# A decoder layer's projections: the products with the weights' high part first, those with the low part last

## The reference

```python
xn = rms_norm(x, attn_norm_w)
q, k, v, qi, ki, wi, cx, cb, cc, ga, gc = split(xn @ w_in)
q, k = rope(rms_norm(q)), rope(rms_norm(k)); qi, ki = rope(qi), rope(ki)
attn = attend(q, k, v, qi, wi, ki)        # keys picked by top-256 of the indexer's scores
conv_out = cb * causal_dwconv([conv_prev, cc * cx], conv_w)
mixed = sigmoid(ga) * (attn @ w_o_attn) + sigmoid(gc) * (conv_out @ w_o_conv)
h = x + mixed @ w_merge
g, val = split(rms_norm(h) @ w_up)
y = h + (silu(causal_dwconv(g) + b) * val) @ w_down
```

## Time and profile before

| | us |
|---|---|
| time, median of 3 runs | 1758.48 |
| lowest and highest run | 1755.22, 1758.77 |
| the profiled execution's own time | 1760.87 |
| its span, first to last instruction | 1759.0 |
| PE busy in the span | 1685.2 |
| DVE busy | 1240.5 |
| ACT busy | 695.2 |
| POOL busy | 879.6 |

### The profile page before, as it was taken

One profiled execution on the slowest core, in us unless ns is written; L12 is line 12 of the kernel. 1 busy time (PEld: TensorE's weight loads), 2 busy tenths in 40 slices (PEclk: granted clock), 3 DMA queues, 4 the chain that ended last, 5 costly groups with the idle time before them and its releaser, 6 DMA issues.

```text
span 1759.0 us, 31969 instructions
## 1 busy us (share of the span) xinstructions
PE 1685.2 (96%) x11519; PEld 1620.4 (92%) x11519; DVE 1240.5 (71%) x1957; ACT 695.2 (40%) x1054; POOL 879.6 (50%) x466
## 2 busy tenths in 40 slices
PE   7999999999999889999799998899999999999999
PEld 5858999999999778898799998899999999999999
DVE  5569999999899655556543378677777776655555
ACT  4755552232111377777212334344444444311110
POOL 2504762455786556755221224666666666633331
PEclk9999999999999889899999999999999999999999
DMA  5221112111776242222333312212222122622222
GB/s 196 83 71 37 36 48 87 60 54 56 267 238 210 67 142 76 85 74 91 114 133 133 142 64 84 73 72 95 72 72 84 72 82 87 240 96 96 96 77 96
DMA packets 66978, 178.32 MB, mean 101 GB/s; under 512 B 15386, under 2 KB 15514, under 8 KB 66762
## 3 DMA queue, kind: packets, MB, share of 16 engines
q1 hardware_dynamic: 56786, 140.91, 24.1%
q10 hardware_dynamic: 9392, 32.10, 4.8%
q0 software_dynamic: 720, 4.29, 0.6%
HBM read 141.79 MB, written 35.58 MB: 101 GB/s over the span
## 4 chain that ended last, share of the span: by engine, by line
PE 75%; DVE 11%; ACT 3%; issue 3%; POOL 3%; SPq 3%; DMA 2%; DVEq 0%; ACTq 0%; POOLq 0%
PE PS L1075 16%; PE PS L663 15%; PE PS L1139 11%; PE PX L1075 6%; PE PS L998 5%; PE PS L1043 5%; PE PX L1139 4%; PE PS L951 3%; DVE S L2108 2%; DVE M L2106 2%; PE PS L921 2%; PE PX L934 2%; DVE LD L2088 2%; PE PS L979 2%; PE PS L766 1%
## 5 line engine op out<-in xcount | busy, mean ns | idle before, releaser
L663 PE MATMUL PS<-XH,WHI 128*128 128x346 f32 (+1 forms) x984 | 321.4, 327 | 6.2 <-POOL WLO L1741 4.9
L663 PE MATMUL PS<-XL,WHI 128*128 128x346 f32 (+1 forms) x984 | 318.1, 323 | 0.0
L663 PE MATMUL PS<-XH,WLO 128*128 128x346 f32 (+1 forms) x984 | 317.5, 323 | 0.0
L1741 POOL TENSOR_TENSOR WLO<-WRAW,WHI 128x1024 fp32r<-128x1024 f32 x58 | 143.7, 2478 | 296.7 <-ACT WHI L1167 296.6
L2108 DVE MATCH_REPLACE8 S<-M,S 128x1024 f32<-128x1024 f32 (+3 forms) x224 | 206.0, 926 | 0.0
L663 PEld LDWEIGHTS PS<-XH,WHI 128*128 128x128 f32 x984 | 186.6, 190 | 16.1 <-issue 9.3
L2106 DVE MAX8 M<-S 128x8 f32<-128x1024 f32 (+3 forms) x224 | 200.7, 931 | 0.4
L663 PEld LDWEIGHTS PS<-XH,WLO 128*128 128x128 f32 x984 | 186.6, 190 | 0.0
L663 PEld LDWEIGHTS PS<-XL,WHI 128*128 128x128 f32 x984 | 186.6, 190 | 0.0
L2382 DVE TENSOR_TENSOR HY<-HY,PS 128x344 f32<-128x344 f32 x198 | 100.9, 513 | 79.2 <-PE PS L1139 79.2
L1139 PE MATMUL PS<-FH,DLO 128*128 128x344 f32 x396 | 126.7, 320 | 0.0
(11 more groups left out here) (369 smaller groups left out, 4821.0 us busy)
## 6 DMA issues: line engine op xcount, KB each, us to landing
WRAW<-wtiles SPq DMA_DIRECT2D x49, 512.0 KB, 3.6
KR<-cache_k SPq DMA_DIRECT2D x64, 256.0 KB, 3.0
RING<-cache_v SPq DMA_DIRECT2D x64, 256.0 KB, 2.9
ffn_act<-TG ACTq DMA_DIRECT2D x22, 516.0 KB, 2.7
FRAW<-ffn_act SPq DMA_DIRECT2D x11, 1032.0 KB, 6.9
RAWG<-wtiles SPq DMA_DIRECT2D x22, 512.0 KB, 3.6
RAWV<-wtiles SPq DMA_DIRECT2D x22, 512.0 KB, 4.4
DRAW<-wdown SPq DMA_DIRECT2D x11, 1024.0 KB, 4.9
```

The lines of the kernel that those rows point to most:

```text
L663: last = nc.tensor.matmul(PS[b][:, c, 0:n], w[b][:, kk, :], x[:, kk, t0 + c * n:t0 + (c + 1) * n], start=(kk == 0 and p == 0), stop=(kk == ...
L1741: nc.gpsimd.tensor_tensor(WLO[b][:, :, :], WRAW[b][:, :, :], WHI[b][:, :, :].bitcast(F32), ALU.subtract).then_inc(w_lo[b], 1)
```

## The change

`proj` waits for the high part of its weights (`w_hi`) where it waited for the low part. It runs the 16 products with the high part for each of the three chunks, 48 in all, then waits for `w_lo`, and then runs the 24 products with the low part, again chunk by chunk. `mid` and `mid1` are still called behind the first and the second chunk of the first loop, so they stand behind 16 and 32 matmuls where they stood behind 24 and 48. Number and shapes of the matmuls are as before.

```diff
-                pe.wait_ge(w_lo[b], k + 1)
+                pe.wait_ge(w_hi[b], k + 1)
                 if not (isinstance(k, int) and k == 0):
                     pe.wait_ge(ps_free[b], k)
                 if extra:
                     extra()
                 for c in range(NCH):
                     for kk in range(kn):
-                        for p, (w, x) in enumerate(((WHI, xh), (WHI, xl), (WLO, xh))):
-                            last = nc.tensor.matmul(PS[b][:, c, 0:n], w[b][:, kk, :], x[:, kk, t0 + c * n:t0 + (c + 1) * n],
-                                                    start=(kk == 0 and p == 0), stop=(kk == kn - 1 and p == 2))
+                        for p, x in enumerate((xh, xl)):
+                            nc.tensor.matmul(PS[b][:, c, 0:n], WHI[b][:, kk, :], x[:, kk, t0 + c * n:t0 + (c + 1) * n],
+                                             start=(kk == 0 and p == 0), stop=False, skip_group_check=True)
                     if c == 0 and mid:
                         mid()
                     if c == 1 and mid1:
                         mid1()
+                pe.wait_ge(w_lo[b], k + 1)
+                for c in range(NCH):
+                    for kk in range(kn):
+                        last = nc.tensor.matmul(PS[b][:, c, 0:n], WLO[b][:, kk, :], xh[:, kk, t0 + c * n:t0 + (c + 1) * n],
+                                                start=False, stop=(kk == kn - 1), skip_group_check=True)
                 last.then_inc(mm[b], 1)
```

## The result

The changed kernel takes 1761.24 us (median of 17 runs: 16 from 1757.68 to 1767.29 us, and a disturbed one of 5312.67 us, which the comparison leaves out); the kernel before, run beside it, 1756.65 us (17 runs, 1752.5 to 1758.89). The ratio is 1.0024 [1.0016, 1.0033]: slower by 0.24%, some 4.2 us. Forecast were 1759.6 us and +1.1 us. The time lies in the range and the sign is right, but the loss is three to four times the forecast, and just beyond the 0.2% within which the forecast called it no change (its likeliest outcome, 0.71). That the time is only 1.6 us from the forecast one is in part luck: before's median is 1756.65 us over 17 runs, 1.83 us under the 1758.48 from which the forecast counted.

A forecast was written before the change was run, and what follows sets the result against it. PE was taken to set the pace until the convolution's results are written, DVE's searches later, to 596 us. -3.33 + 0.3 + 2.56 + 1.55 = +1.1 us on the median 1758.48 gave 1759.6 us, range 1756.0 to 1763.0.

The forecast's parts named there:

- Part one: PE's wait at 142.28 us: 1.87 us goes by the moved `weigh_past`, 1.46 by the slow clock behind it; 3.33 gained.
- Part two: The eight `head_sums` move up 8 matmuls and may wait for ACT's squares; 0.3 us lost.
- The early gain: PE's time saved before 437 us brings key pages and DVE forward; 3.0 us, DVE's result at 595.5 instead of 598.5.
- slower rival: The gain before the first key pages never reaches DVE, which ends at 598.5 as before; 1762.6 us, chance 0.16.
- Part four: Behind DVE's last result: 40 matmuls instead of 24 follow `decode_logits`, 2.56 us, and an earlier slow clock, 1.55; 4.1 lost.
- Part three: Removing the low-part waits at 459.31 and 576.08 us is worth nothing: PE only waits longer for DVE, 8.7 us.
- Faster: Rival: all four low-part waits (4.93 us) and two slow stretches come off in full; 7.9 us, 1750.6, chance 0.09.
- Nothing happens: Rival: the low part is almost always there first, gain and loss each under a microsecond; 1758.5 us, chance 0.09.

The follow-up runs named there:

- e4: The changed kernel (new order, moved guests), but with the low part waited for ahead of the whole projection; ratio 1.0000 against the kernel before.
- e7: The kernel before, with the new order only in the one projection that holds `weigh_past`; ratio 0.9987 against the kernel before.
- e1: The kernel before, with the new order only in the last projection; ratio 1.0019 against the kernel before.
- e9: The kernel before, old order throughout, with `decode_logits` behind the whole last projection and SP's wait for POOL's last key product; ratio 0.9988.
- e5: The changed kernel again, nothing altered; ratio 1.0020 against the kernel before.
- e10: The kernel before, unchanged, profiled a second time without timed runs; 1761.52 us.
- e11: The kernel before, unchanged, profiled a third time without timed runs; 1755.57 us.
- e2: The changed kernel, with the old order in the last projection alone; ratio 0.9976 against the kernel before.
- e3: The changed kernel, with `mid` and `mid1` kept behind 24 and 48 products as before; ratio 0.9980 against the kernel before.
- e6: The changed kernel, with 36 matmuls whose results nobody reads ahead of the waits in `decode_logits`; ratio 1.0006 against the kernel before.
- e8: The changed kernel, with `decode_logits` behind the whole last projection and SP's wait for POOL's last key product; 1750.53 us against 1756.53 before.

## Why the prediction was right in sign and too small

**Part one (-3.33) held.** Both mechanisms are there: the wait goes by the moved guest alone (e4, e7), and the slow stretch behind it follows in all three profiles of before. e7 measured -3.1 us (standard error 0.8), -1.4 of it at full level (1.87 forecast) and -1.7 by the clock (1.46 forecast). But in e1 and e9, whose code is the same at this place, the stretch is missing. If it comes by chance, in three of five, the term is 1.87 + 0.6 x 1.46 = 2.7 on the average; five profiles don't settle that.

**Part two (+0.3) was nothing.** Squares and their sums of after, timelines of ACT and PE, against the earlier trace rows:

```profile
169.68 1.06 ACT L1308 ACTIVATE SQ<-PS 128x1056 f32<-128x1056 f32 x1
```

```profile
170.81 1.36 PE L805 MATMUL PX<-SQ,SELC 128*16 128x352 f32 x6
```

The sums start 0.07 us behind the squares, the room of 0.08 us that was worked out, the projections of this row keep their period of 13.0 us, and PE's waits list none for the other seven.

**The early gain reaches DVE,** so the slower rival's condition is refuted. From the start of the projection that holds `weigh_past` to DVE's first key page it is 329.3 us in all three profiles of before, 327.2 and 327.7 in e1 and e9 (old order without the slow stretch), and 325.7 to 326.7 in the eight with the new order there. PE then reaches `decode_logits` when forecast: counted from the same start, at 586.8 us in after (594.90 - 6.28 - 1.85) and in e5. But DVE comes earlier than forecast, so the pause is 6.3 us rather than 8.7. Counted so, its masking (L2128) starts 4.3 us earlier than in before, and 5.1 in e5, where 3.0 were forecast: 3.3 by the first key page, and 0.9 and 1.7 because it waits less for the last pages. DVE's waits for key pages from 440 to 600 us, before and after (us in total, times, longest):

```profile
DVE LD L2088 <- POOL KR L1868: 12.7, 5, 8.3
```

```profile
DVE LD L2093 <- POOL KR L1873: 9.3, 4, 5.9
```

The prediction took the 1.71 us of the earlier trace rows and its like as they were; one such wait is gone. In after the masking itself was shorter too (last section).

**Part four (+4.1) held in its sum.** Way from `decode_logits` to `decode_turn`, PE's 24 products left: 15.05, 16.6, 15.05, 16.5, 17.4, 12.3 us (before, e10, e11, e2, e3, e7), 15.5 on the average. With 40 left: 20.1, 19.4, 20.2, 19.0, 19.1 (after, e5, e1, e4, e6), 19.6: +4.1. In e1, where nothing else is changed, it cost 3.5 us. Its two terms were less exact. With 40 left, the profiles that begin at half clock take 19.9 us (after, e5, e1) and those that begin at full clock 19.05 (e4, e6): 0.9 for the early fall instead of 1.55. With 24 left, those that begin at full clock behind a pause take 15.8 (before, e10, e11, e2): 3.2 us for the 16 products, part of them at half clock, instead of 2.56.

**Part three (0) is the step that failed.** The prediction said of the waits at 459 and 576 us that their removal is "worth nothing", since PE only waits longer for DVE. At full level this is right. But the longer pause isn't free. e4, which has everything of the change but the split of the wait, ends at +0.4 us, the sum of e7 and e1 (-3.1 + 3.5). Taking the two late waits away as well, which is the changed kernel, adds 3.3 us (each kernel against the runs of before on its own chip; standard error some 1.1), by the lower level (+3.8 against +0.2). Filling the pause in e6 takes that away. The pauses are 2.62 us in e4 and 6.3 to 6.6 in after and e5. With shorter pauses the "nothing" of part three holds: e2 and e3 take the late waits away as well and pause for 3.80 and 3.56 us, and they are as fast as e7 (-3.6 and -3.1 against -3.1), which keeps them. The sum had one price for the pause, the 1.55 us of part four with a bound of 1.5 more, and none for what part three added to it.

**What stays open** is where the whole of these 3.8 us lies. I summed (1 - clock) over stretches of 5 us in each profile, from 20 to 1750 us (none is lost from 160 to 430):

| us | 20 to 115 | 115 to 160 | 430 to 580 | 580 to 625 | 625 to 1750 | all |
|---|---|---|---|---|---|---|
| before, e10, e11 (mean) | 2.8 | 1.7 | 1.4 | 7.9 | 23.7 | 37.5 |
| after, e5 (mean) | 5.1 | 0 | 0 | 10.4 | 23.8 | 39.2 |
| e4 | 3.4 | 0 | 1.7 | 9.6 | 22.9 | 37.6 |
| e6 | 5.1 | 0 | 0 | 8.4 | 20.7 | 34.2 |

Around `decode_logits` the changed kernel loses 2.5 us more than before, part four's share in it, and 2 us more than with the pause filled. But against e4, which has the same products there and the shorter pause, it is 0.8 us, and e1 with a pause of 3.84 us loses 10.8. So most of the 3.3 us is not seen at the place where the pause is. Another 2.3 us lie ahead of 115 us, where it makes projections too; but e10 and e1, with the old order there, have 5.1 as well, so the change need not cause it. Behind 625 us one profile differs from the next by up to 4 us whatever the kernel. The timed runs show the sum and that it goes with the pause filled; single profiles are too few to place it all.

**The rivals.** Faster (PE's waits count in full) is refuted: PE waits for DVE, as said. "Nothing happens" is refuted by e1 and e2, each a change of 0.2% and of opposite sign. The loss that the slower rival named came out nearly in size (+4.1 forecast, +3.7 and +4.2 measured), by another mechanism: the early gain did reach DVE, and the clock took as much back.

## What to carry to other kernels

When work is reordered around a call that waits for another engine, count what stands behind that wait: here 16 products moved behind it cost 0.19%, and moving the call behind all of them gained 0.32% with the rest of the change. A wait saved on an engine that will wait anyway need not be free: it lengthens a pause, and a longer pause can cost some of TensorE's clock (here 3.3 us at 6.3 to 6.6 us of pause, nothing that shows in e2 and e3 at 3.6 to 3.8). A time that one profile shows behind a wait (the slow stretch at 142 us) should be looked at in several before it is counted in full.

## What the runs showed of the hardware

A longer pause had its price from the first matmul: in the profiles with pauses of 1.33 to 2.62 us, `decode_logits` began at full clock; with 6.3 and 6.6 us at half. In between it went both ways: at full behind 3.80 us (e2), at half behind 3.84 (e1) and 3.56 (e3).

DVE's masking of the scores was held up by POOL. Groups of after and of e8 (line, engine, operation, shapes | busy us, mean ns | idle before):

```profile
L2128 DVE TENSOR_SCALAR S<-S 128x1024 f32<-128x1024 f32 x1 | 2.9, 2892 | 0.0
L2128 DVE TENSOR_SCALAR S<-S 24x1056 f32<-24x1056 f32 x1 | 0.7, 700 | 0.0
```

```profile
L2130 DVE TENSOR_SCALAR S<-S 24x1056 f32<-24x1056 f32 x1 | 3.0, 2979 | 0.0
...
L2130 DVE TENSOR_SCALAR S<-S 128x1024 f32<-128x1024 f32 x1 | 0.7, 674 | 0.0
```

POOL's subtractions beside it (`HKL`, L1829 of before), in before and in e8:

```profile
595.51 2.44 POOL L1829 TENSOR_TENSOR HKL<-QKT,HKH 64x1056 fp32r<-64x1056 f32 x1 [0.27 <-POOL HQ L1825]
```

```profile
592.80 2.43 POOL L1836 TENSOR_TENSOR HKL<-QKT,HKH 64x1056 fp32r<-64x1056 f32 x1 [0.28 <-POOL HQ L1832]
```

The same 24x1056 operation takes 0.70 us in after and 2.98 in e8 (2.34 in before), and the next one the other way round. In before, e2, e4, e5, e6 and e8 it began while the subtraction ran, and whenever that was, it ended 0.56 to 0.57 us behind the subtraction's end (before: 598.51 and 597.95; e8: 595.79 and 595.23). In after it began 0.15 us ahead of the subtraction (593.74 and 593.89) and took its 0.70 us. So in most of these profiles it is POOL's subtraction that decides when `decode_logits` may start; the luck of the order in after makes some 1.3 us of the 3.7 by which it starts earlier than in before (the long form, 2.34 us, would have ended at 596.08, and PE waited until 594.76 for ACT).

The Trainium skill, page "SBUF — State Buffer", section "🔬 SBUF: two separate sides", says that GpSimd shares a pair of ports with some of VectorE's operations, that whichever starts first has the pair for its whole instruction, and that the other waits. The durations agree with it; that the masking is such an operation is not shown otherwise.
